# Two attention output projections by seven quarter products instead of eight, with the weight sums on GpSimd

## What is computed

```
# first block
mix = concatenate([o_a, o_b], axis=-1)          # (512, 1024), 16 heads of 64
h = h + mix @ w_out                             # w_out (1024, 1024)
hn = rms_norm(h, norm2_g)                       # then the gated feed-forward layer

# second block, its second layer (only the 512 latent tokens go on)
m_l = attention_output @ od_w_out               # (512, 1024) @ (1024, 1024)
x = x + mod_l[2] * m_l                          # mod_l[2]: one gate value per output column
f = moe(modulate(x, norm_ffn, ...))             # then the mixture of experts
```

## Time and profile before

| | us |
|---|---|
| median of 3 runs | 2046.06 |
| lowest and highest run | 2043.63, 2049.18 |
| the profiled execution, span | 2041.3 |
| busy in it: PE, DVE, ACT, POOL | 1919.5, 1113.7, 643.1, 250.0 |
| first block: attention, then projection (PE from its first to its last matmul) | 204 to 320.6, then 320.6 to 378.4 |
| second block, second layer: attention, then projection | 1646.7 to 1767.7, then 1767.7 to 1825.5 |

### The profile page before, as it was taken

How to read it: one execution, slowest core, us unless ns; L and a number is a source line. 1 busy time by engine, 2 the same in 40 slices (tenths; PEclk the granted TensorE clock), 3 DMA queues, 4 the chain that set the end, 5 groups by cost and what they waited for, 6 DMA issues and landing times.

```text
span 2041.3 us, 28960 instructions
## 1 busy us (share of the span) xinstructions
PE 1919.5 (94%) x11010; PEld 1050.4 (51%) x11010; DVE 1113.7 (55%) x1860; ACT 643.1 (32%) x1274; POOL 250.0 (12%) x260
## 2 busy tenths in 40 slices
PE   7999999999999999999999999899997999999993
PEld 4544875544444444555655774543335578645330
DVE  2001772387787401257773652667765757457774
ACT  2011661200000000242222650346652656323551
POOL 3000110011111100002200001611102000041101
PEclk9999999999999999999999999999998989999997
DMA  8633101477666421410210102679967020039995
GB/s 264 160 83 124 54 12 42 144 247 260 224 240 245 147 101 41 131 40 12 83 42 1 63 2 84 243 313 340 357 257 260 1 83 2 35 130 371 380 418 197
DMA packets 105559, 318.11 MB, mean 156 GB/s; under 512 B 8967, under 2 KB 42919, under 8 KB 86992
## 3 DMA queue, kind: packets, MB, share of 16 engines
q1 hardware_dynamic: 75008, 184.79, 25.2%
q0 software_dynamic: 25168, 112.53, 15.5%
q10 hardware_dynamic: 5248, 18.94, 2.3%
HBM read 285.72 MB, written 35.76 MB: 157 GB/s over the span
## 4 chain that ended last, share of the span: by engine, by line
PE 74%; issue 8%; DVE 6%; DMA 5%; PEld 5%; PEldq 1%; ACT 1%; POOL 1%; DVEq 0%; ACTq 0%; POOLq 0%; SPq 0%
PE ps L3081 15%; PE ps L2512 7%; PE ps L358 7%; PE ps L1703 6%; PE ps L329 6%; PE ps L833 5%; PE ps L879 4%; PE ps L2882 4%; PE ps L854 4%; PE ps L2533 3%; PE ps L1679 2%; DMA X<-moe_rows,row_token 2%; PEld ps L1426 2%; PE ps L1426 1%; PE ps L2504 1%
## 5 line engine op out<-in xcount | busy, mean ns | idle before, releaser
L3081 PE MATMUL ps<-wide 128*128 128x512 f32 (+1 forms) x736 | 306.5, 575 | 1.9 <-issue 1.7
L3081 PEld LDWEIGHTS ps<-wide 128*128 128x128 f32 x736 | 138.3, 190 | 166.2 <-issue 164.1
L2512 PE MATMUL ps<-wide,X 128*32 x448 | 199.2, 598 | 2.1 <-DVE X L2683 2.1
L2512 PE MATMUL ps<-Z,X 128*32 128x512 f32 x1344 | 199.6, 598 | 0.0
L1703 PE MATMUL ps<-wide 128*128 128x512 f32 (+1 forms) x384 | 148.9, 544 | 0.5 <-issue 0.5
L1187 DVE SCALAR_TENSOR_TENSOR Z<-Z,wide 128x2048 f32<-128x2048 f32 x56 | 131.6, 2350 | 2.8
L833 PE MATMUL ps<-T 64*128 64x256 f32 (+1 forms) x888 | 109.7, 377 | 8.7 <-DVE nm L972 6.8
L1426 PE MATMUL ps<-wide 128*128 128x512 f32 x256 | 113.8, 602 | 2.1 <-issue 1.0
L2512 PEld LDWEIGHTS ps<-wide,X 128*32 128x32 f32 x448 | 47.2, 110 | 125.4 <-issue 125.4
L393 ACT ACTIVATE T<-ps 128x512 f32<-128x512 f32 (+2 forms) x139 | 70.8, 537 | 129.3 <-PE ps L1426 111.5
L904 ACT ACTIVATE T<-T,nm 128x768 f32<-128x768 f32 (+3 forms) x112 | 86.7, 775 | 77.3 <-DVE nm L972 77.3
(11 more groups left out here) (408 smaller groups left out, 3380.9 us busy)
## 6 DMA issues: line engine op xcount, KB each, us to landing
wide<-in_experts SPq DMA_DIRECT2D x64, 1024.0 KB, 9.5
Z<-in_mod_w POOLq DMA_DIRECT2D x32, 1024.0 KB, 5.3
T<-in_experts SPq DMA_DIRECT2D x32, 1024.0 KB, 11.5
X<-in_mod_w POOLq DMA_DIRECT2D x16, 1024.0 KB, 5.5
moe_out<-X ACTq DMA_DIRECT2D x28, 512.0 KB, 8.4
wide<-in_w_gate SPq DMA_DIRECT2D x22, 512.0 KB, 5.4
wide<-in_w_up SPq DMA_DIRECT2D x22, 512.0 KB, 6.5
wide<-in_w_in SPq DMA_DIRECT2D x10, 1024.0 KB, 10.4
```

The costliest lines, as they stand in the source:

```text
L2512: last = pe.matmul(ps[rows, t % 2, :], mo.xT[:, c, rows], w_rows, start=(c == 0), stop=(c == DK - 1))
L3081: last = pe.matmul(self.gu.bank(u)[:, columns], w, self.rhs(c)[:, columns], start=(c == 0), stop=(c == DK - 1))
```

## The change

`Linear` is replaced in the two places by a new stage `OutBySeven`. The 512 tokens, the 1024 contraction rows and the 1024 output columns are each cut in two, which makes quarters of the activations (256 tokens by 512), of the weights (512 by 512) and of the output (256 by 512). The four output quarters are made of seven products of quarters instead of eight, after sums of quarters. In the code's names (h and l are the high and the low token half; b11 to b22 the weight quarters as loaded):

- weight sums, on GpSimd, each of 128x2048: t3, the new content of b12, t2 and t4. t3 and t2 take two ring slots of their own, so the projection now holds all six (`pass_over`); t4 lies in the context tiles of `k.X`. In the second block the four loaded quarters are multiplied by the gate row first (four more operations of 128x2048, with the gate row repeated four times by a stride of 0), which takes the gate out of the additions;
- activation sums, 128x1024 each: s3 on GpSimd (`differ`), s1, s2 and s4 on VectorE at the start of the projection's stage;
- seven products P1 to P7, each two parts (one per token tile of 128), each part 4 matmuls of 128x512: 56 matmuls. P1 and half of P7 (12 matmuls) are in `begin`;
- VectorE adds each part to every output quarter that it belongs to: 20 additions to `k.X`, 8 of them 1024 columns wide (the bank read twice), each waiting for the one before.

In the first block GpSimd makes the four weight sums behind its bias loads number 2 to 5, and s3 behind the fourth; in the second block it makes the eight operations in a row at the start of the attention stage, as soon as the four quarters have landed. Releases of ring slots: two at the first matmul of P4, two at the first of P2, one at the second part of P3, one at the end.

```diff
+class OutBySeven(Stage):
+    ADDS = ("P7", 0, "l"), ("P7", 1, "l"), *((p, i, row) for p, rows in (("P1", "hl"), ("P4", "l"), ("P5", "hl"), ("P6", "hl"))
+                                               for i in range(2) for row in rows), *((p, i, "h") for i in range(2) for p in ("P2", "P3"))
+    BANKS = {"P1": 0, "P7": 2, "P4": 4, "P5": 6, "P6": 0, "P2": 4, "P3": 6}
...
+    def blend(self, pool, i):
+        k, rg = self.k, self.k.rg
+        if i == 0:
+            for n in (self.b11, self.b12, self.b21, self.b22):
+                rg.await_landed(pool, n)
+            pool.wait_ge(k.weights_used, self.t2 - SLOTS + 1)
+        else:
+            pool.wait_ge(k.weights_blended.sem, self.blends + i)
+        if i < self.steps - 4:
+            w = rg.slot((self.b11, self.b12, self.b21, self.b22)[i]).rearrange("p (c n) -> p c n", c=4)
+            g = self.gate[:, 512 * (i % 2):512 * (i % 2) + 512].unsqueeze(1).to_broadcast((P, 4, 512))
+            pool.tensor_tensor(w, w, g, ALU.mult).then_inc(k.weights_blended.sem, 1)
+            return
...
+        pool.tensor_tensor(out, a, b, ALU.subtract).then_inc(k.weights_blended.sem, 1)
...
+    def tensor(self, pe):
+        k, rg = self.k, self.k.rg
+        self.part(pe, "P7", 1, self.s3, rg.slot(self.t3))
+        for i in range(2):
+            self.part(pe, "P4", i, self.quadrant(1, 0), self.t4, 0 if i else 2)
+        self.after_sum(pe, "S1")
+        for i in range(2):
+            self.part(pe, "P5", i, self.s1, rg.slot(self.b12))
+        self.after_sum(pe, "S2")
+        self.after_add(pe, "P1", 1, "l")
+        for i in range(2):
+            self.part(pe, "P6", i, self.s2, rg.slot(self.t2))
+        self.after_sum(pe, "S4")
+        self.after_add(pe, "P5", 1, "l")
+        for i in range(2):
+            self.part(pe, "P2", i, self.quadrant(1, 1), rg.slot(self.b21), 0 if i else 2)
+            self.part(pe, "P3", i, self.s4, rg.slot(self.b22), i)
+            if i == 0:
+                self.norm.turn(pe, 0)
...
@@ PairAttention.gpsimd
             pool.wait_ge(k.bias_used.sem, self.b_used + q - 1)
             self._load(pool, q)
+            if q < 6:
+                self.then.blend(pool, q - 2)
+            if q == 5:
+                pool.wait_ge(k.packs_scaled.sem, self.mul + self.before)
+                self.then.differ(pool)
+        if isinstance(self.then, OutBySeven) and not self.loads:
+            for i in range(self.then.steps):
+                self.then.blend(pool, i)
+            pool.wait_ge(k.packs_scaled.sem, self.mul + self.before)
+            self.then.differ(pool)
...
-        projection.early.then = Linear(k, hT, DK, A["w_out"][0], D, seq, residual, ["dve"] * 8, norm=[(seq, gain(1), None)])
+        projection.early.then = OutBySeven(k, A["w_out"][0], [(seq, gain(1), None)], T[:, 10240:11264])
...
-        odd.then = Linear(k, hT, DK, A["od_w_out_2"][0], D, seq, gated_take(oddgate), ["dve"] * 8, norm=mod_sets(1, 1, False))
+        odd.then = OutBySeven(k, A["od_w_out_2"][0], mod_sets(1, 1, False), k.Z[:, 7680:8704], oddgate[:, 0, :])
```

More of the change, by code:

```diff
@@ L268, in load, with pass_over @@
             sp.dma_start(place(self.slot(n)), src).then_inc(self.k.landed[n % SLOTS], 16)
+    def pass_over(self, n):
+        self.loads += [None] * n
+        self.landed_at += [0] * n
+        return len(self.loads) - n
     def lend(self, loads):
@@ L3309, in two_blocks @@
         k.both_done = tally("both_done")
+        k.weights_blended, k.halves_differed = tally("weights_blended"), tally("halves_differed")
+        k.sums_made, k.partials_added, k.parts_full = tally("sums_made"), tally("partials_added"), tally("product_parts_full")
         k.mods_ready = sem("mods_ready")
```

98 lines of the change are left out of this document (added).

## The result

| | before | after |
|---|---|---|
| time, median (runs) | 2046.65 us (5) | 2052.86 us (5) |
| lowest to highest | 2043.63 to 2049.18 | 2050.70 to 2055.54 |
| span of the profiled execution | 2041.3 us | 2050.7 us |

The ratio is 1.0031, with a 95% interval of 1.0018 to 1.0043: 3.7 to 8.8 us slower. Taking 16 matmuls out made the kernel slower, by about what the forecast said (2050.9). The profile of before is of its fastest execution (2043.63 us), the profile of after is of its median one, so the two spans differ by 9.4 us and the medians by 6.2.

A forecast was written before the change was run, and what follows sets the result against it. TensorE, busy 94%, was taken as the bound. Matmuls -13.8, gate off additions -0.7, bank wait +2.3, half clock +1.7, GpSimd holding VectorE in second attention +10.8 and first +4.5: +4.8, so 2050.9 us, range 2041 to 2059.

The follow-up runs named there:

- e3_gated: The changed kernel with each GpSimd weight operation placed right behind a spread copy of a pack; 2039.64 us, ratio to before 0.9965.
- e6_both: The changed kernel with the weight operations moved as in e3_gated and VectorE's additions of P1 put first; 2037.78 us, ratio to before 0.9953.
- e4_pieces: The changed kernel with each GpSimd weight operation cut into four of 512 columns at the same places; 2041.76 us, ratio to before 0.9979.
- e9_halves: e6_both with each of GpSimd's two operations per stored row tile cut into two of 512 columns; 2038.19 us, ratio to before 0.9962.

## What to carry to other kernels

Before work goes to an idle GpSimd, list VectorE's instructions beside it that copy within SBUF or read two SBUF tensors, and who waits for them: each may stand as long as one GpSimd instruction, or several that follow without a gap, however small it is itself. Put long GpSimd instructions right behind such an instruction; the same work then held nothing in the attentions here, and 16 matmuls less became a gain of 6.7 (e3_gated) to 7.8 us (e6_both). Cutting them is less sure: it cost nothing in one attention and 2.8 us in the other. Where a chain of small VectorE operations met a backlog of GpSimd, cutting didn't help.

## What the runs showed that was not expected

- An idle of 2.0 us of PE was followed by 6.8 us at half clock in one execution and none in another, with the same code; one of 3.26 us by none, one of 3.88 by 3.4 us. In one stage this is worth 3.7 us, about as much as the first block's whole gain (3.9), so a single profile can't price a change of this size.
- Between two GpSimd instructions without a gap a held VectorE instruction sometimes gets in (second attention of e4_pieces, at most 1.31 us) and sometimes doesn't: L682 of e9_halves stood through two until a gap of 0.08 us (3.56 us), L1139 of e4_pieces through four until GpSimd was done (4.33 us). L1139 had begun 0.39 us ahead of the end of a piece, and one that did get in (L1187) 0.49 ahead, so having begun doesn't tell them apart. Why is open.
- A GpSimd operation of 128x2048 took some 4.55 us (4.50 to 4.63 in after) with two different inputs, 3.68 with one tensor as both inputs and output, and a copy 1.96.
